# The front of a hybrid decoder block in two halves of the model width

## The chip, the cores and the metric

The kernel runs on one core of a Trainium2 chip. The metric is the device time of one execution in microseconds, from a program's start to its end; lower is better. The core has five engines that run side by side, each with its own instruction order: TensorE (PE) for matrix products and transposes, VectorE (DVE), ScalarE (ACT), GpSimd (POOL) and SyncE (SP), which issues nearly all of the DMA transfers. Engines wait for each other by semaphores.

## What is computed

The reference is one residual layer for 1024 positions and a model width of 1024, in float32:

```python
mod = (silu(c) @ w_ada + b_ada)                     # 6 rows of 1024
sh1, sc1, g1, sh2, sc2, g2 = split(mod, 6)
h = rms_norm(x, norm1_g) * (1 + sc1) + sh1
proj = h @ w_in                                     # q 512, k 128, v 128, u 512 columns
q = rope(rms_norm(q, q_norm_g), cos, sin)           # angles = positions * inv_freq
k = rope(rms_norm(k, k_norm_g), cos, sin)
attn = sliding_window_attention(q, k, v, sinks)     # window 128
pooled = means of u over the last 2, 4, 8, 16 positions, minus u
pool_out = (pooled @ pool_w per group) * pool_scale
x = x + g1 * (concat(attn, pool_out) @ w_o)
h2 = rms_norm(x, norm2_g) * (1 + sc2) + sh2
x = x + g2 * (square(relu(h2 @ w1)) @ w2)
```

For this document the part that matters is everything up to the first projections: the rows shift 1 (`sh1`) and scale 1 (`sc1`) must be computed from the vector `c` and two parts of `w_ada` of 4 MB each before any `h` exists, and `h` is needed before the first product with `w_in`.

## The kernel before

**Tiles.** The positions are cut in 8 tiles of 128 (`NT` = 8, `P` = 128), the model width in 8 blocks of 128 (`KD` = 8, `NK` = 4 of them are a half). Products are made in three parts to keep float32 accuracy: every operand is split in a high part (`hi`, a cast on ScalarE or GpSimd to a rounded format) and a low part (`lo`, what the cast lost, a subtraction on VectorE), and TensorE adds hi·hi, lo·hi and hi·lo. So the weights `w_in` have `wih` and `wil`, in two column groups: `wu` (the 512 columns of u, 4 pieces of two blocks each) and `wqkv` (768 columns, 8 pieces of one block each); and each tile's `h` has a high and a low part in two halves of 512 of the model width.

**The modulation rows.** `w_ada`'s rows lie over the 128 partitions, 8 to a partition. VectorE runs over 8 pieces of 128x1024 per modulation row: `add_piece` multiplies a piece by a column of silu(c) and adds it (L1205 for the first piece, L1207 for the others) to an accumulator: `acc` for `sh1`, `acc_sc` (in the tile `squares`) for `sc1`. Each add counts up `mod_summed`. What is left is a sum over partitions: TensorE multiplies the accumulator's eight blocks by a column of ones (`column_sum`, L2076), one column in each, and VectorE adds the bias and makes `b1` and `a1`, per-partition shift and scale for the transposed x (`scale_1`, L1269 and L1272). Later modulation rows (the "jobs" sh2, sc2, g1, g2) are summed in the same way between the tiles' work by lists of piece numbers (`first_pieces`, `between_pieces`, `late_pieces`), all in `acc`, and turned at tiles 3 and 5.

**x.** ScalarE squares a tile (`square_x`, L720), GpSimd makes 1/rms (`root_x`, L1872), ScalarE scales (`scale_x`, L725), TensorE transposes (`turn_x`, L2056), and VectorE (`make_h`, L1281) and ScalarE (`make_h_half`, L734) apply `a1` and `b1` to one half each. `hi_h` (L744) casts, `lo_h` (L1287) subtracts; `h_hi` and `h_lo` count these.

**Order.** Every engine's instructions stand in the order in which its block of the program is written. SyncE loads the pieces of the list `stream` one after another into 12 buffers (4 named `raw`, 8 named `slots`), and each load waits until its buffer was used. In the kernel before the list is: 8 of sh1, 8 of sc1, 4 of wu, 8 of wqkv; the tiles x 0 and x 1 are loaded behind piece 7. VectorE sums in that order, then makes the low parts of the weights (`lo_wu` L1294, `lo_wqkv` L1300). The rotary angles (`angles`, L1215 to L1234) are made after the first q is there, and their sines on ScalarE. TensorE sums the columns of sh1 right when they are ready, transposes x 0 and x 1, and fills the time until sc1 is ready with transposes that nobody reads (`keep_clock(n, bank)`, n multiplications with the identity, L2073; in the profile one such multiplication is two records). Then it sums the columns of sc1, and the projections start: u of tile 0, q and kv of tile 0, u of tile 1 and so on, over the whole width. `pool_windows` (L2200) and `pool_out` (L2173) are the pooling branch, `turn_qk` the transposes of the first queries and keys. From tile 2 on one loop runs over the tiles.

**GpSimd** builds the pooling matrices `band` with selects (`band_of`, L1858 and L1861, and L1866), among them the special first 16 columns of tile 0, which it overwrites again when tile 0 is done.

## Time and profile before

| | us |
|---|---|
| median of 3 runs | 937.73 (936.92 to 937.75) |
| the profiled execution, in all | 939.17 |
| its span, first to last instruction | 937.4 |
| TensorE busy in the span | 915.0 (98%) |
| VectorE busy | 650.2 (69%) |
| ScalarE busy | 495.1 (53%) |
| GpSimd busy | 361.7 (39%) |
| mean granted TensorE clock | 0.996 |

The profile was taken of one execution, whose own time is 1.4 us above the median of the runs without one; 1.7 us of it lie around the span. TensorE is the engine to look at: in all of the span's forty slices but the first and the last its busy digit is 9. The first slice, 23 us long, is where it is mostly idle. A row of the timeline gives an instruction's start, its length, engine, line, operation, what it writes and reads, the count of like instructions in a row, and in brackets the idle time of the engine ahead of it with what ended that. Ends of matmuls are modelled, so the time from one start to the next is the better measure of a matmul's cost. The granted clock is the share of full speed: 1.00 is 2.4 GHz, 0.50 is 1.2 GHz.

### The profile page before, as it was taken

How to read it: one execution, taken by the hardware profiler on the slowest of the kernel's cores; microseconds unless marked ns; L12 is line 12 of the kernel's file. 1: busy time of each engine (PE TensorE's matmuls, PEld its weight loads, DVE VectorE, ACT ScalarE, POOL GpSimd, SP SyncE). 2: the span in 40 equal slices, each digit the busy share in tenths (PEclk: the TensorE clock that was granted, in tenths of full speed). 3: DMA queues.
4: the chain of work that ended last, by engine and by line, in shares of the span. 5: the costliest groups of instructions: out<-in, count | busy, mean ns of one | idle time of the engine just before them, and what ended most of it. 6: DMA issues, size and time to landing. Idle time of an engine off the chain costs nothing.

```text
span 937.4 us, 12606 instructions
## 1 busy us (share of the span) xinstructions
PE 915.0 (98%) x4387; PEld 765.5 (82%) x4387; DVE 650.2 (69%) x1001; ACT 495.1 (53%) x869; POOL 361.7 (39%) x347
## 2 busy tenths in 40 slices
PE   2999999999999999999999999999999999999998
PEld 2888888887888888888888888888888888888886
DVE  6978987888645778556555654445786666799896
ACT  2657888887655546554455544536334444333331
POOL 8162322243323446988888888721000000000000
PEclk9899999999999999999999999999999999999999
DMA  9943232235122423746555553349999538996772
GB/s 357 371 170 95 91 114 90 91 106 188 45 90 90 134 69 123 243 162 197 188 176 169 176 184 131 115 172 332 349 339 320 196 102 289 317 302 209 258 248 94
DMA packets 92271, 175.54 MB, mean 187 GB/s; under 512 B 9320, under 2 KB 26288, under 8 KB 92208
## 3 DMA queue, kind: packets, MB, share of 16 engines
q1 hardware_dynamic: 92096, 174.70, 55.0%
q8 instruction: 35, 0.57, 0.2%
q14 instruction: 28, 0.23, 0.1%
q10 hardware_dynamic: 112, 0.04, 0.0%
HBM read 136.95 MB, written 37.75 MB: 186 GB/s over the span
## 4 chain that ended last, share of the span: by engine, by line
PE 92%; DVE 4%; DMA 2%; SPq 1%; issue 1%; ACT 1%; POOL 0%; DVEq 0%
PE psum L2060 27%; PE psum L2062 27%; PE psum L2061 27%; PE psum L2056 3%; DMA raw<-in_w_ada 2%; PE psum L2154 1%; PE psum L2155 1%; PE psum L2158 1%; PE psum L2140 1%; DVE w_o_lo L1372 1%; PE psum L2230 1%; PE psum L2200 1%; PE psum L2173 1%; PE psum L2236 1%; DVE probs L1337 1%
## 5 line engine op out<-in xcount | busy, mean ns | idle before, releaser
L1115 ACT CAST down_operands<-down_raw 128x1024 fp32r<-128x1024 f32 x96 | 100.9, 1054 | 151.9 <-PE psum L2062 54.6
L2060 PE MATMUL psum<-down_operands 128*128 128x512 f32 x448 | 174.3, 389 | 0.0
L2061 PE MATMUL psum<-down_operands 128*128 128x512 f32 x448 | 174.3, 389 | 0.0
L2062 PE MATMUL psum<-down_operands 128*128 128x512 f32 x448 | 174.3, 389 | 0.0
L1775 DVE TENSOR_TENSOR down_operands<-down_raw,down_operands 128x1024 fp32r<-128x1024 f32 x93 | 112.5, 1220 | 19.5 <-ACT down_operands L1115 18.9
L2060 PE MATMUL psum<-h2T,w_operands 128*128 128x512 f32 x272 | 106.0, 390 | 0.1
L2062 PE MATMUL psum<-h2T,w_operands 128*128 128x512 f32 x272 | 105.9, 389 | 0.0
L2061 PE MATMUL psum<-h2T,w_operands 128*128 128x512 f32 x272 | 105.8, 389 | 0.0
L2060 PEld LDWEIGHTS psum<-down_operands 128*128 128x128 f32 x448 | 84.1, 188 | 17.6
L2062 PEld LDWEIGHTS psum<-down_operands 128*128 128x128 f32 x448 | 84.1, 188 | 17.4
L2061 PEld LDWEIGHTS psum<-down_operands 128*128 128x128 f32 x448 | 84.1, 188 | 17.3
L2012 POOL TENSOR_TENSOR w_operands<-raw,w_operands 128x512 fp32r<-128x512 f32 x56 | 84.2, 1505 | 35.6 <-ACT w_operands L1063 35.6
L2062 PE MATMUL psum<-t_sums_hi,w_operands 128*128 128x512 f32 x168 | 65.4, 389 | 0.0
L2060 PE MATMUL psum<-t_sums_hi,w_operands 128*128 128x512 f32 x168 | 65.4, 389 | 0.0
L2061 PE MATMUL psum<-t_sums_lo,w_operands 128*128 128x512 f32 x168 | 65.4, 389 | 0.0
L2060 PEld LDWEIGHTS psum<-h2T,w_operands 128*128 128x128 f32 x272 | 51.1, 188 | 11.1 <-issue 0.5
L2061 PEld LDWEIGHTS psum<-h2T,w_operands 128*128 128x128 f32 x272 | 51.1, 188 | 10.6
L2012 POOL TENSOR_TENSOR w_operands<-w_sums,w_operands 128x512 fp32r<-128x512 f32 x42 | 55.3, 1329 | 11.3 <-ACT w_operands L1063 11.3
L2062 PEld LDWEIGHTS psum<-h2T,w_operands 128*128 128x128 f32 x272 | 51.1, 188 | 10.5
L1063 ACT CAST w_operands<-w_sums 128x512 fp32r<-128x512 f32 x42 | 26.1, 623 | 55.9 <-PE psum L2062 52.5
L2060 PE MATMUL psum<-w_o_hi,mixT_hi 128*128 128x512 f32 x128 | 51.2, 400 | 0.0
L2062 PE MATMUL psum<-w_o_hi,mixT_lo 128*128 128x512 f32 x128 | 50.0, 391 | 0.0
(285 smaller groups left out, 1960.9 us busy)
## 6 DMA issues: line engine op xcount, KB each, us to landing
down_raw<-in_w_mlp_out SPq DMA_DIRECT2D x160, 256.0 KB, 4.3
down_raw<-act_scratch SPq DMA_DIRECT2D x112, 256.0 KB, 3.3
raw<-in_w_ada SPq DMA_DIRECT2D x32, 512.0 KB, 4.6
raw<-in_w_mlp_in SPq DMA_DIRECT2D x32, 512.0 KB, 5.0
act_scratch<-act_quads_a SPq DMA_DIRECT2D x64, 256.0 KB, 2.3
act_scratch<-act_quads_b SPq DMA_DIRECT2D x48, 256.0 KB, 3.6
slots<-in_w_ada SPq DMA_DIRECT2D x8, 512.0 KB, 10.6
xh<-in_x SPq DMA_DIRECT2D x8, 512.0 KB, 5.7
```

Of the source, the lines that this page charges most:

```text
L1063: nc.scalar.copy(w1op[:, w1_slot(b, name), 0, :, :], w1_quad(b, quad)).then_inc(w1_hi, 1)
L1115: nc.scalar.copy(o[:, 0, :, :], r[:, 0:2, :]).then_inc(op2_hi, 1)
L1337: ins = v.tensor_tensor_reduce(out=pr[:, kv, h, 0:w], in0=banks(4)[:, 256 * h:256 * h + w], in1=mask[:, m0:m0 + w], scale=1.0, scalar=-3e3 ...
L1372: v.tensor_tensor(wol[:, k, :], piece_at(place[("wo", k)]), woh[:, k, :].bitcast(F32), ALU.subtract).then_inc(wo_lo_dve, 1)
L1775: v.tensor_tensor(o[:, 1, :, :], r[:, 0:2, :], f32(o[:, 0, :, :]), ALU.subtract).then_inc(op2_lo_dve, 1)
L2012: g.tensor_tensor(o[:, 1, :, :], quad, o[:, 0, :, :].bitcast(F32), ALU.subtract).then_inc(w1_lo, 1)
L2056: return nc.tensor.transpose(o, i, ident[0:rows_, 0:rows_])
L2060: mm(o, wh, ah, start=first, stop=False, skip_group_check=adds)
L2061: mm(o, wh, al, start=False, stop=False, skip_group_check=adds)
L2062: return mm(o, wl, ah, start=False, stop=last, skip_group_check=adds)
L2140: ins = mm(o, qT[:, kv * G + h, :], k_, start=a == 0, stop=a == 1)
L2154: mm(bank(0), h[:, k, :], wih[:, k, QKV:IN], start=k == 0, stop=False)
```

## The change

What it does:

1. The first job is cut along the model width. The list `stream` now begins with 8 pieces of kind `mod`, each with the first 512 columns of shift 1 and the first 512 of scale 1 of one row block (two runs of 2 KB in each partition where there was one of 4 KB). Then come wu 0 and 1, wqkv 0 to 3, the second halves (`mod` 8 to 15), wqkv 4 to 7, wu 2 and 3. x 0 is loaded behind piece 2, x 1 behind wu 1; x 2 and x 3 behind the parameter rows.
2. VectorE sums the first halves in `acc` (shift left, scale right) and the second in `squares` (`sum_front`), the last piece of each in two cuts of 512. The cast of the positions stands behind piece 2 of the first half, the columns' copy and `angles` behind piece 3; `angles` makes its products with one instruction from a row of constants (`inv_row`) that GpSimd sets, where it had eight.
3. TensorE projects the first half of the width for tile 0 and tile 1 (u in banks 0 and 1, q in 6 and 4, kv in 3 and 5), then the second half of both. In the two gaps ahead of a half it runs fills, 27 and 8 in the first, 11 in the second, and eight column sums.
4. The high parts of wu 1, wqkv 1 and wqkv 3 are cast on GpSimd instead of ScalarE. The matrix of tile 0's first 16 columns gets a tile of its own (`band_first`), with four narrow products more in `pool_windows(0)`, and nothing is overwritten later. GpSimd makes the roots of x 0 and x 1 one by one.
5. The jobs sh2, sc2 and g1 have an accumulator each, their pieces come later in the lists, and their turns move from tiles 3 and 5 to tiles 4 and 6.

The core of the diff:

```diff
-        stream = [("sh1", k) for k in range(KD)]
-        stream += [("sc1", k) for k in range(KD)]
-        stream += [("wu", k) for k in range(KD // 2)]
-        stream += [("wqkv", k) for k in range(KD)]
+        stream = [("mod", k) for k in range(KD)]
+        stream += [("wu", 0), ("wu", 1)]
+        stream += [("wqkv", k) for k in range(NK)]
+        stream += [("mod", KD + k) for k in range(KD)]
+        stream += [("wqkv", k) for k in range(NK, KD)]
+        stream += [("wu", 2), ("wu", 3)]
...
-        JOB_LOADS = (4, 4, 4, 3, 4, 4, 1, 0)
+        JOB_LOADS = (4, 2, 3, 4, 4, 5, 2, 0)
+        job_sums = (slots[:, NT - 1, :], slots[:, NT - 2, :], acc[:, :])
+        POOL_CASTS = ((1,), (1, 3))
...
+            if kind == "mod":
+                half = k // KD
+                return wada[:, k % KD, 0:2 * D].rearrange("p (m d) -> p m d", m=2)[:, :, 512 * half:512 * half + 512]
...
             for n in range(first_job):
                 load(n)
-                if n == 7:
+                if n == 2:
                     load_x(0)
+                if n == place[("wu", 1)]:
                     load_x(1)
-            load_x(2)
...
+            load_x(2)
+            load_x(3)
...
             def load_x(t):
                 if t >= 2:
-                    sp.wait_ge(h_lo, 2 * (t - 1))
+                    sp.wait_ge(h_lo, h_step(t - 2, 1))
```

VectorE:

```diff
+            def sum_front(half):
+                sums = acc_sc if half else acc
+                for k in range(KD):
+                    if k >= 1:
+                        dve.wait_ge(mod_summed, front_summed(KD * half + k - 1))
+                    if k < KD - 1:
+                        add_piece(sums[:, :], ("mod", KD * half + k), k, mod_summed)
+                    else:
+                        a = landed(dve, ("mod", KD * half + k))
+                        for m in range(2):
+                            cut = slice(512 * m, 512 * m + 512)
+                            v.scalar_tensor_tensor(out=sums[:, cut], in0=a[:, cut], scalar=silu[:, k:k + 1],
+                                                   in1=sums[:, cut], op0=ALU.mult, op1=ALU.add).then_inc(mod_summed, 1)
+                    if half == 0 and k == 1:
+                        dve.wait_ge(rows_in, 16 * 4)
+                        v.tensor_copy(rows[64:72, :], posi[64:72, :]).then_inc(posf_ready, 1)
+                    if half == 0 and k == 2:
+                        dve.wait_ge(rows_turned, 1)
+                        v.tensor_copy(cols[:, :], psum[:, 0, 0:72]).then_inc(cols_ready, 1)
+                        angles()
+                    if half == 1 and k == 1:
+                        lo_h(1, 0)
...
-            first_pieces = ([], [], (5,), (8,), (12, 13), (16,), (18, 19), (22,))
-            between_pieces = ([], [], [], (9,), (14,), (17,), (20,), (23,))
-            late_pieces = ((0, 1, 2, 3), (4,), (6, 7), (10, 11), (15,), [], (21,), [])
+            first_pieces = ([], [], (2,), (5,), (9,), (13, 14), (18,), (22,))
+            between_pieces = ([], [], [], (6,), (10,), (15,), (19,), (23,))
+            late_pieces = ([], (0, 1), (3, 4), (7, 8), (11, 12), (16, 17), (20, 21), [])
```

TensorE:

```diff
+            for n, fill in ((3, 8), (4, 7)):
+                pe.wait_ge(mod_summed, n)
+                keep_clock(fill, 3)
+            turn_x(0)
+            for n, fill in ((5, 3), (6, 5), (7, 4)):
+                pe.wait_ge(mod_summed, n)
+                keep_clock(fill, 3)
             pe.wait_ge(mod_summed, KD)
-            for k in range(KD):
-                ins = column_sum(psum[:, k // 4, k % 4:k % 4 + 1], acc, k)
+            for k in range(NK):
+                ins = column_sum(bank(1)[:, k:k + 1], acc, k)
             ins.then_inc(mod_turned, 1)
-            turn_x(0)
-            pe.wait_ge(cols_ready, 1)
-            turn_x(1)
-            keep_clock(3, 2)
-            for n, fill in ((13, 4), (14, 4), (15, 2)):
+            pe.wait_ge(mod_summed, KD + 1)
+            for k in range(NK):
+                ins = column_sum(bank(2)[:, k:k + 1], acc, NK + k)
+            ins.then_inc(sc1_turned, 1)
+            keep_clock(8, 3)
...
+            project_u_half(0, 0)
+            turn_x(1, 0, NK)
+            project_qkv_half(0, 0, (q_part(0), kv_part(0)))
+            project_u_half(1, 0)
+            project_qkv_half(1, 0, (q_part(1), kv_part(1)))
+            keep_clock(4, 2)
+            for n, fill in ((15, 4), (16, 3)):
                 pe.wait_ge(mod_summed, n)
                 keep_clock(fill, 2)
+            for m in range(2):
+                pe.wait_ge(mod_summed, 2 * KD + 1 + m)
                 for k in range(NK):
+                    ins = column_sum(bank(2)[:, NK * m + k:NK * m + k + 1], acc_sc, NK * m + k)
+            ins.then_inc(sc1_turned, 1)
+            pe.wait_ge(b1_second, 1)
+            pe.wait_ge(a1_ready, 2)
+            turn_x(1, NK, KD)
+            project_qkv_second()
+            project_u_half(0, 1)
+            project_u_half(1, 1)
+            pe.wait_ge(u_kept, 1)
+            turn_x(2)
+            project_qkv_half(1, 1, (q_part(1),))
             pool_windows(0)
-            turn_x(2)
-            pe.wait_ge(q_gained, 1)
-            project(bank(6), 0, AW, 1).then_inc(q_done, 1)
+            project_qkv_half(1, 1, (kv_part(1),))
             pool_out(0)
```

On TensorE, the stretch from the last fills ahead of the last column sums to the first product of u. `mod_summed` counts VectorE's adds, `ones` is the column of ones; before:

```order
L2073 MATMUL psum<-ident 128x128 [waits mod_summed]
L2073 MATMUL psum<-ident 128x128
L2076 MATMUL psum<-ones,squares 128x1 [waits mod_summed]
L2076 MATMUL psum<-ones,squares 128x1 x3
L2076 MATMUL psum<-ones,squares 128x1 [waits mod_summed]
L2076 MATMUL psum<-ones,squares 128x1 x3
L2073 MATMUL psum<-ident 128x128 [waits mod_taken]
L2073 MATMUL psum<-ident 128x128 x3
L2230 MATMUL psum<-w_in_hi,hT_hi 128x512 [waits wu_hi,h_hi]
```

and after:

```order
L2145 MATMUL psum<-ident 128x128 [waits mod_summed]
L2145 MATMUL psum<-ident 128x128 x3
L2148 MATMUL psum<-ones,acc 128x1 [waits mod_summed]
L2148 MATMUL psum<-ones,acc 128x1 x3
L2148 MATMUL psum<-ones,acc 128x1 [waits mod_summed]
L2148 MATMUL psum<-ones,acc 128x1 x3
L2145 MATMUL psum<-ident 128x128 x8
L2309 MATMUL psum<-w_in_hi,hT_hi 128x512 [waits wu_hi,cols_ready,h_hi]
```

The eight sums are now of half the shift and half the scale, and the fills behind them are eight and wait for nothing.

On TensorE after the change, the gap between the two halves; the rows ahead of it are the last products of the first half of tile 1, the rows behind it the second half of q and kv of tile 0. No such place is there before:

```order
L2315 MATMUL psum<-w_in_lo,hT_hi 128x256
L2145 MATMUL psum<-ident 128x128 x4
L2145 MATMUL psum<-ident 128x128 [waits mod_summed]
L2145 MATMUL psum<-ident 128x128 x3
L2145 MATMUL psum<-ident 128x128 [waits mod_summed]
L2145 MATMUL psum<-ident 128x128 x2
L2148 MATMUL psum<-ones,squares 128x1 [waits mod_summed]
L2148 MATMUL psum<-ones,squares 128x1 x3
L2148 MATMUL psum<-ones,squares 128x1 [waits mod_summed]
L2128 MATMUL psum<-ident,xh 128x128 [waits x_scaled,a1_ready,b1_second]
L2128 MATMUL psum<-ident,xh 128x128 x3
L2309 MATMUL psum<-w_in_hi,hT_hi 128x512 [waits wqkv_hi,h_front_hi]
```

Between a product of the first half and one of the second now stand 11 fills, eight column sums and four transposes of x tile 1, with three waits for VectorE's sums and one for shift and scale.

On VectorE, from the second piece to the point at which the first sums are done; `rows_in` counts the small rows (biases, gains, positions) that arrive on ScalarE's queue. Before, piece 2 to the columns' copy:

```order
L1207 SCALAR_TENSOR_TENSOR acc<-raw,small,acc 128x1024 [waits raw_in1,mod_summed]
L1207 SCALAR_TENSOR_TENSOR acc<-raw,small,acc 128x1024 [waits raw_in2,mod_summed]
L1207 SCALAR_TENSOR_TENSOR acc<-raw,small,acc 128x1024 [waits raw_in3,mod_summed]
L1207 SCALAR_TENSOR_TENSOR acc<-slots,small,acc 128x1024 [waits raw_in4,mod_summed]
L1251 CAST probs<-probs 8x128 [waits rows_in]
L1207 SCALAR_TENSOR_TENSOR acc<-slots,small,acc 128x1024 [waits raw_in5,mod_summed]
L1207 SCALAR_TENSOR_TENSOR acc<-slots,small,acc 128x1024 [waits raw_in6,mod_summed]
L1207 SCALAR_TENSOR_TENSOR acc<-slots,small,acc 128x1024 [waits raw_in7,mod_summed]
L1255 COPY cols<-psum 128x72 [waits rows_turned]
```

and after:

```order
L1257 SCALAR_TENSOR_TENSOR acc<-raw,small,acc 128x1024 [waits raw_in1,mod_summed]
L1300 CAST probs<-probs 8x128 [waits rows_in]
L1257 SCALAR_TENSOR_TENSOR acc<-raw,small,acc 128x1024 [waits raw_in2,mod_summed]
L1304 COPY cols<-psum 128x72 [waits rows_turned]
L1264 TENSOR_TENSOR probs<-cols,probs 128x64 [waits ident_made,cols_ready]
L1268 TENSOR_SCALAR probs<-probs 128x64 [waits own_dve]
L1270 TENSOR_SCALAR probs<-probs 128x64 [waits own_dve]
L1273 SCALAR_TENSOR_TENSOR probs<-probs 128x64 [waits own_dve] x3
```

The wait for the small rows moved from behind piece 5 to behind piece 2, and the angles from behind the first q to behind piece 3.

## Rows read from the trace of the kernel before

**Rows 1.** The page: busy time, the chain that ended last, one group of DMA issues.

```profile
PE 915.0 (98%) x4387; PEld 765.5 (82%) x4387; DVE 650.2 (69%) x1001; ACT 495.1 (53%) x869; POOL 361.7 (39%) x347
...
PE 92%; DVE 4%; DMA 2%; SPq 1%; issue 1%; ACT 1%; POOL 0%; DVEq 0%
...
down_raw<-act_scratch SPq DMA_DIRECT2D x112, 256.0 KB, 3.3
```

**Rows 2.** Waits of TensorE from 60 to 240 us: total, times, longest.

```profile
PE psum L2056 <- DVE kT L1367: 0.5, 1, 0.5
```

**Rows 3.** Timeline of TensorE and its weight loads: start, length, line, in brackets idle.

```profile
20.57 3.68 PE L2056 MATMUL psum<-ident,xh 128*128 128x128 f32 x16 [0.81 <-ACT xh L725]
...
26.29 0.97 PEld L2073 LDWEIGHTS psum<-ident 128*128 128x128 f32 x8 [0.35 <-DVE squares L1207]
...
28.39 1.95 PE L2076 MATMUL psum<-ones,squares 128*128 128x1 f32 x16
...
31.95 2.07 PE L2230 MATMUL psum<-w_in_hi,hT_hi 128*128 128x512 f32 x4 [0.61 <-ACT hT_hi L744]
...
40.38 0.50 PE L2230 MATMUL psum<-w_in_hi,hT_hi 128*128 128x512 f32 x2
...
47.80 0.51 PE L2230 MATMUL psum<-w_in_hi,hT_hi 128*128 128x512 f32 x2
...
48.85 0.40 PE L2154 MATMUL psum<-w_in_hi,hT_second 128*128 128x512 f32 x1
...
54.31 1.14 PE L2200 MATMUL psum<-band,u_rows 128*128 128x144 f32 x8
55.28 1.04 PE L2056 MATMUL psum<-ident,xh 128*128 128x128 f32 x8
...
65.41 0.81 PE L2056 MATMUL psum<-ident,qkn 128*128 128x128 f32 x6
```

**Rows 4.** Windows: length; busy PE, PEld, DVE, ACT, POOL; granted clock, DMA share, GB/s.

```profile
26.00:28.00 2.00, 1.68 (x13) 1.36 (x12) 1.93 (x3) 0.00 (x0) 1.88 (x3) 1.00 1.03 385
31.00:32.00 1.00, 0.39 (x5) 0.20 (x3) 0.96 (x4) 0.90 (x3) 0.00 (x0) 0.64 1.07 398
32.00:33.00 1.00, 1.00 (x3) 0.81 (x4) 1.00 (x2) 1.00 (x4) 0.00 (x0) 0.50 1.03 399
38.00:39.00 1.00, 1.00 (x5) 0.77 (x4) 1.00 (x2) 1.00 (x3) 0.00 (x0) 0.95 1.03 402
```

**Rows 5.** Timeline of VectorE.

```profile
6.35 1.28 DVE L1207 SCALAR_TENSOR_TENSOR acc<-raw,small,acc 128x1024 f32<-128x1024 f32 x1 [0.53 <-DMA raw<-in_w_ada]
...
11.97 0.22 DVE L1251 CAST probs<-probs 8x128 f32<-8x128 int32 x1
...
27.59 1.42 DVE L1247 SCALAR_TENSOR_TENSOR squares<-raw,small,squares 128x512 f32<-128x512 f32 x2
...
51.71 0.20 DVE L1220 TENSOR_SCALAR probs<-probs 128x64 f32<-128x64 f32 x1
...
53.66 0.20 DVE L1234 TENSOR_SCALAR probs<-probs 128x64 f32<-128x64 f32 x1
...
149.66 1.39 DVE L1366 TENSOR_TENSOR qT<-psum,qT 64x512 fp32r<-64x512 f32 x2 [1.62 <-ACT kT L817]
```

**Rows 6.** Issue of the last small row; loads issued from 2 to 3 us, time to landing.

```profile
3.74 0.36 ACTq L713 DMA_DIRECT2D probs<-in_positions  x1
...
raw<-in_w_ada SPq DMA_DIRECT2D x3, 512.0 KB, 5.7
```

**Rows 7.** Timeline of ScalarE.

```profile
31.80 1.50 ACT L734 ACTIVATE xh<-psum,small 128x128 f32<-128x128 f32 x4
```

**Rows 8.** Timeline of GpSimd.

```profile
10.74 1.25 POOL L1861 TENSOR_SCALAR_AFFINE_SELECT band<-band 128x16 f32<-128x16 f32 x1
...
16.98 0.20 POOL L1861 TENSOR_SCALAR_AFFINE_SELECT band<-band 128x16 f32<-128x16 f32 x1
...
201.97 1.04 POOL L1918 CAST w_o_hi<-raw 128x1024 fp32r<-128x1024 f32 x1 [5.62 <-PE psum L2062]
```

482 lines of the change are left out of this document (259 added, 223 removed).

## The prediction

> **What bounds the kernel now.** I read the page's busy shares and chain first: TensorE works in 98% of the span, and 92% of the chain that ended last is TensorE [rows 1]. The waits of the matmul queue from 60 to 240 us are four, 1.3 us together; the longest, 0.5, is for the low half of a key tile [rows 2]. So a microsecond taken out of the front counts in full, and one added counts in full. Next comes TensorE's timeline of the front [rows 3]. The first product starts at 31.95, and the transposes of the first queries and keys (turn_qk of tile 0) at 65.41. Both programs do the same work before that transpose, so its start is my yardstick. The windows [rows 4] show the third thing: the granted clock falls in the slice from 31 (0.64), is 0.50, the 1.2 GHz level, in the six whole microseconds behind it (the first is shown), and is back (0.95) in the slice from 38; before and after it is 2.4 GHz. The 24 products of u for tile 0 took from 31.95 to about 40.4, 8.43 us; the same 24 for tile 1 took 48.85 to 54.31, 5.46 us [rows 3]. The low clock costs the kernel before 3.0 us.
>
> What did the engine do before the clock fell? From 28.39 it ran the eight column sums, 1.95 us, which stream one column each; then four fills; then it was idle for 0.61 us [rows 3].
>
> **Part 1, the early start.** The new first job is eight pieces holding the first 512 columns of shift and scale. VectorE takes 1.28 us a piece [rows 5]. The pieces are cut in 2 KB rows instead of 4 KB. The nearest rows are the stretch in which the projection weights, also in 2 KB rows, arrive: 385 GB/s [rows 4], that is 1.36 us for 512 KB. VectorE, with its work of 1.30 a piece and what is added below, sets this stretch. It now waits for the small rows after piece 2. The last of them is issued at 3.74 to 4.10, and loads issued in that microsecond took 5.7 us to land [rows 6]; VectorE reached the same instruction only at 11.97 and did not wait [rows 5]. The wait ends between 7.8, where VectorE is ready anyway, and 9.8; I take 8.6, since these rows are small. With the cast and piece 3: 10.15. Then the angles: nine steps from 51.71 to 53.86 and a first one of 0.25 [rows 5], 2.4 us, and the copy of the columns 0.23: 12.8. They cost nothing where they stood, since TensorE's rows behind them, at 54.31 and 55.28, show no idle time [rows 3]; here they are on the path. Four pieces of 1.30 and two halves of 0.71 [rows 5]: the first sums stand at 18.7 and 19.4.
>
> TensorE's fills must not be late for them. A fill is two records in the profile and costs 0.24 us at the high clock (eight loads, four fills, in 0.97). The sixteen transposes from 20.57 ran at 0.23 us each, eight at 55.28 at 0.13 [rows 3]; at the slower of these rates a fill costs 0.43. The eight fills at 10.2 are done by 12.1 or 13.6, in any case before piece 4 is added at 14.1. The remaining 19 fills and eight transposes (0.87) take 5.5 us from 14.1 to 19.6, 0.9 us after the first half sum is ready, so the first column sums end at 20.6, the second at 21.6 (eight in 1.95, [rows 3]). Scale and bias: 0.45. ScalarE's four activations 1.50 [rows 7] and a cast 0.62: the first product starts at **24.2**, 7.7 us earlier. If the fills and transposes run at the slow rate up to there, add 1.5 us.
>
> **Part 2, the first half of the products.** Half of u is 12 products at 0.2275 us (5.46 / 24): 2.73. Half of q and kv is four steps of 1.05 (47.80 to 48.85): 4.2 [rows 3]. Two tiles: 13.9 us, and four transposes of x tile 1, 0.45. Tile 1's scaling waits for ScalarE's square (1.25), GpSimd's root (two small steps; I take 0.8) and the scaling (1.15) behind tile 0's cast: 27.65, against 27.0 on TensorE, a wait of 0.65. The casts of weights 1 and 3 go to GpSimd. A cast of 1024 columns took it 1.04 us [rows 8], so 0.8 for 768. The upper end is 2.1, with a VectorE instruction (1.28) in its way: the same select took 1.25 us beside VectorE's sums and 0.20 without [rows 8]. With the upper value VectorE ends its four low parts at 31.5, with the lower at 30.4; TensorE's fourth step is due at 31.3, so the cover just holds, and if it does not it is 0.2. First half done: 24.2 + 13.9 + 0.45 + 0.65 = **39.2**.
>
> **Part 3, the gap between the halves.** VectorE: 0.75, six pieces of 1.30, lo_h of tile 1 0.61, two halves 1.42: 10.6 us after 31.5, so 42.1. (The loads would allow 36.2: from a first landing at 5.1, sixteen pieces and two of wu at 1.36, two x tiles at 1.28, four of wqkv at 0.99, and 1.4 for the last piece's sum.) TensorE runs 11 fills, 2.7 us, to 41.9, then eight column sums, 1.95: 43.85. Shift and scale 0.5, two transposed blocks on VectorE 0.7 (four took ScalarE 1.50, [rows 7]), a cast of 256 columns 0.4: TensorE resumes at **45.6**. Of 6.4 us between the halves nothing is useful work. That is the price of the early start.
>
> **Part 4, to the yardstick.** q and kv of tile 0 4.2 and 0.35 of waiting for its low half; u twice, 5.46; then keep_u(0), which stands on ScalarE behind the square and scaling of x tile 2. That load now waits for three low halves (47.4) and lands after 3.3 (the fastest loads on the page, [rows 1]) to 5.7 us [rows 6]; I take 5.0, so u is kept at 56.2 and TensorE waits 0.6. Transposes 0.87, q of tile 1 2.73, pool windows 1.2 (0.97 from 54.31 to 55.28 [rows 3], plus four narrow matmuls), kv 1.45, pool products 0.9. Together 17.8: **63.4** at the high clock throughout, against 65.4 before. So the reordering gives 2.0 us, with the high clock granted everywhere.
>
> **Part 5, the steady part.** Three modulation pieces less before tile 2, three more behind it, and the two transposes of sums go from tiles 3 and 5 to 4 and 6. VectorE's path to the low part of q and k changes by -1.0, +0.2, +1.3 and +0.4 us at tiles 3 to 6 (pieces of 1.28 moved across it). At tile 5 it stood still 1.62 us ahead of that low part before [rows 5], and TensorE is 0.9 us later itself at tiles 4 and 6. I take 0, bounds -0.5 and +0.5 (its longest wait there, [rows 2]). The band that was mended after tile 0 (12 small GpSimd steps) goes away off the path: 0. The loads of x tiles 2 and 3 on SyncE now stand behind the parameters, and the job loads behind both; the first job piece is used only after norm_k(1): 0.
>
> **The clock, where I had to choose.** What preceded the fall at 31.3 is found twice in the new program: 1.95 us of column sums before each restart. At the second one no fill follows them; they are joined by the 1.6 us of shift, scale and cast in which TensorE has nothing but four transposes. At the first, eight fills follow, and 19 stand ahead. By the rows, the second restart is emptier than the stretch that preceded the fall before, so I expect the fall there: 3.0 us lost, of which waits of 0.35 and 0.6 in that stretch swallow about 0.5. At the first restart I take the high clock, as the fills are denser than before.
>
> The Trainium skill (TensorE: Matmul & The Clock Gate, "HAM oscillation — how this bites in real kernels") puts such falls down to idle gaps, waits for data between bursts of matmuls. By that rule the new gaps, each under 2 us of idleness and filled, would leave the clock high, and the sum would be the 935.7 of the first rival below; this trace speaks against it, since the clock fell behind column sums and one idle piece of 0.61 us.
>
> **The sum.** -2.0 (Parts 1 to 4) + 0 (Part 5) + 2.5 (one fall) = +0.5 us. The profiled execution took 939.17 with a span of 937.44, so 1.73 lie around the span; its plain runs have a median of 937.73. The sum makes the span 937.9, the profiled execution 939.7, and the median 937.73 + 0.5 = **938.2**.
>
> **The rivals.**
> First, the clock stays high over both restarts. For it: 19 and 11 fills and a split of the first column sums. Against it: 3.6 us in the second gap without any fill. It gives -2.0: 935.7.
> Second, the other side: the clock falls at both restarts. The first fall costs 3.0 less the 0.65 of waiting in the first half, 2.4 us. For it: 1.95 us of column sums and 0.7 us of nothing ahead of the first product, as before. Against: more fills. It decides only where TensorE and not VectorE ends the first half: beyond 0.65 us of loss every further one counts until the first half ends after 39.2, and from there it moves the whole second half, since 11 fills then run into the column sums. Total +2.9: 940.6.
> Third, the change brings no early start, because the small rows or GpSimd's root come late (upper bounds of Parts 1 and 2): up to 2 us later at 24.2, all of it kept. With one fall, 940.2.
>
> **How the numbers follow.** Chances: one fall 0.38, none 0.35, two 0.22, late start or anything else 0.05. Each case has about 1.3 us either way (0.8 from the small rows, 0.8 from the load of x tile 2 and the casts, 0.5 from Part 5, not all at once). The range reaches from 935.7 - 1.3 = 934.4 to 940.6 + 0.6 = 941.2; the likeliest case alone would be 936.9 to 939.5. A measurement of this kernel can tell about 0.2%, 1.9 us, from no change: faster is below 935.85, half of the first rival and a little of the likeliest and of the unknown, 0.27; slower is above 939.6, most of the second and third rivals and a little of the likeliest, 0.26; within is 0.47.
>
> **What would show it.** First product near 24.2 and the yardstick at 63.4 plus the half-clock loss. Part 1 is wrong if the first column sums begin away from 19.6; Part 2 if the first half ends away from 39.2, or if products wait for the casts of GpSimd; Part 3 if VectorE's last half sum is not near 42.1 or the restart not near 45.6; the clock choice if the granted clock does not fall near the second restart, or falls near the first. The prediction fails as a whole if the stretch behind the yardstick does not have the length that it had before.

## The result

The changed kernel takes 940.32 us (median of 10 runs, 938.43 to 941.34), the kernel before 937.11 us (10 runs, 936.56 to 937.75). The ratio is 1.0031, 95% interval 1.0022 to 1.0041: 0.31% slower, 2.9 us by the ratio and 3.2 between the two medians. The prediction said 938.2 with a range of 934.4 to 941.2 and 0.26 for slower by over 0.2%. So the range held, the likeliest value was 2.1 us too low, and the case that came is one to which I gave a quarter. For the profiled executions the forecast was closer: 939.7, and 940.24 came.

### The profile after

The page of the changed kernel, its busy times and its chain [rows 1]:

```profile
PE 919.8 (98%) x4453; PEld 770.5 (82%) x4453; DVE 647.8 (69%) x988; ACT 495.8 (53%) x875; POOL 353.7 (38%) x331
...
PE 92%; DVE 4%; ACT 1%; issue 1%; DMA 1%; POOL 1%; ACTq 0%; DVEq 0%
```

TensorE works 4.8 us more, in a span that is 1.1 us longer: what was added are 29 fills (46 in the two gaps against 17 before) and four narrow products. Its timeline of the front (the columns as in [rows 3]):

```profile
10.55 3.78 PE L2145 MATMUL psum<-ident 128*128 128x128 f32 x16 [0.87 <-DVE acc L1257]
14.53 2.66 PE L2145 MATMUL psum<-ident 128*128 128x128 f32 x14 [0.19 <-DVE acc L1257]
17.02 1.04 PE L2128 MATMUL psum<-ident,xh 128*128 128x128 f32 x8
...
20.57 1.84 PE L2148 MATMUL psum<-ones,acc 128*128 128x1 f32 x16
22.28 2.03 PE L2145 MATMUL psum<-ident 128*128 128x128 f32 x16
25.06 1.20 PE L2309 MATMUL psum<-w_in_hi,hT_hi 128*128 128x512 f32 x4 [0.75 <-ACT hT_hi L785]
...
34.93 1.20 PE L2312 MATMUL psum<-w_in_hi,hT_second 128*128 128x512 f32 x4 [0.45 <-DVE hT_second L1351]
...
40.66 2.62 PE L2145 MATMUL psum<-ident 128*128 128x128 f32 x22
43.11 1.84 PE L2148 MATMUL psum<-ones,squares 128*128 128x1 f32 x16
45.52 0.63 PE L2128 MATMUL psum<-ident,xh 128*128 128x128 f32 x4 [0.57 <-DVE small L1317]
46.73 2.70 PE L2309 MATMUL psum<-w_in_hi,hT_hi 128*128 128x512 f32 x8 [0.58 <-ACT hT_hi L792]
...
65.82 0.82 PE L2128 MATMUL psum<-ident,qkn 128*128 128x128 f32 x6
```

Read it against the forecast. The first column sums start at 20.57 (19.6 was forecast), the first product at 25.06 (24.2), the first half ends at 40.66 (39.2), the second column sums start at 43.11, products resume at 46.73 (45.6), and turn_qk(0), the yardstick, starts at 65.82 (63.4 at the high clock, 65.9 with the fall). The two waits of the second gap, 0.57 and 0.58, and the 0.45 ahead of the product with tile 1's low half, are all there is of idle time behind the first product but for some 0.3 us ahead of the transposes of x tile 1.

The windows of the changed kernel (columns as in [rows 4]) show where the granted clock fell:

```profile
47.00:48.00 1.00, 1.00 (x5) 0.83 (x5) 1.00 (x2) 1.00 (x3) 0.00 (x0) 0.51 0.06 16
...
50.00:51.00 1.00, 1.00 (x6) 0.86 (x5) 1.00 (x2) 1.00 (x4) 0.00 (x0) 0.78 0.88 328
```

It fell to 1.2 GHz once, right behind the second restart, as the forecast had chosen, but for 3.4 us (from 47.02, by the 0.51, to 50.44, by the 0.78) and not for the 6.8 us of [rows 4].

VectorE (columns as in [rows 5]):

```profile
8.96 0.22 DVE L1300 CAST probs<-probs 8x128 f32<-8x128 int32 x1 [0.85 <-DMA probs<-in_positions]
...
13.20 1.27 DVE L1257 SCALAR_TENSOR_TENSOR acc<-raw,small,acc 128x1024 f32<-128x1024 f32 x1
...
18.55 1.42 DVE L1296 SCALAR_TENSOR_TENSOR acc<-slots,small,acc 128x512 f32<-128x512 f32 x2
...
41.39 1.41 DVE L1296 SCALAR_TENSOR_TENSOR squares<-slots,small,squares 128x512 f32<-128x512 f32 x2
```

The small rows let it go at 8.96 (8.6 was forecast), the piece behind the angles began at 13.20 (12.8), the first sums stood at 19.3 and 20.0 (18.7 and 19.4) and the second half's at 42.8 (42.1).

So VectorE's steps were met within 0.7 us. TensorE's first column sums came 1.0 us late and the first half took 0.6 us more (15.6 for 15.0), and yet the yardstick is where the forecast with one fall had it, 65.8 for 65.9: the fall cost less than I had put down for it, and the errors cancelled. That match is luck. The experiments say where the 2.1 us of the median come from.

### The profile page after: what moved, and what is told of

Its sections match the earlier page's. It is cut to its first block, busy times and chain, and to the rows that moved or that the text cites. A ratio compares the mean times of both kernels' runs of the same rounds, so it can differ in the third digit from the quotient of the medians.

```text
span 938.5 us, 12724 instructions
## 1 busy us (share of the span) xinstructions
PE 919.8 (98%) x4453; PEld 770.5 (82%) x4453; DVE 647.8 (69%) x988; ACT 495.8 (53%) x875; POOL 353.7 (38%) x331
## 4 chain that ended last, share of the span: by engine, by line
PE 92%; DVE 4%; ACT 1%; issue 1%; DMA 1%; POOL 1%; ACTq 0%; DVEq 0%
PE psum L2132 26%; PE psum L2134 26%; PE psum L2133 26%; PE psum L2128 3%; PE psum L2213 1%; PE psum L2145 1%; PE psum L2312 1%; PE psum L2229 1%; PE psum L2309 1%; PE psum L2230 1%; PE psum L2233 1%; PE psum L2315 1%; DVE w_o_lo L1441 1%; PE psum L2249 1%; DVE probs L1406 1%
## 5 line engine op out<-in xcount | busy, mean ns | idle before, releaser
L2134 PE MATMUL psum<-t_sums_hi,w_operands 128*128 128x512 f32 x168 | 65.4, 389 | 0.0
L2132 PE MATMUL psum<-t_sums_hi,w_operands 128*128 128x512 f32 x168 | 65.4, 389 | 0.0
L2133 PE MATMUL psum<-t_sums_lo,w_operands 128*128 128x512 f32 x168 | 65.4, 389 | 0.0
```

Of the source, the lines that this page charges most:

```text
L2132: mm(o, wh, ah, start=first, stop=False, skip_group_check=adds)
L2133: mm(o, wh, al, start=False, stop=False, skip_group_check=adds)
L2134: return mm(o, wl, ah, start=False, stop=last, skip_group_check=adds)
```

## The experiments

All came from three questions. What is different between the executions? What holds the first column sums? What does the steady part cost? My theory after the first traces: TensorE's rate, and not the terms of the sum, makes most of the difference between forecast and time, and the turn that moved from tile 3 to tile 4 makes 0.8 us. The rival: the new order itself is longer on VectorE, in the front and in the steady part. The times of each comparison are against the kernel before on the same chip.

Two numbers are read from each trace and collected here, with the start of the first column sums and the first product: the distance from those sums to the start of turn_qk(0), and the distance from turn_qk(0) to turn_qk(6), which stands for the steady part. (The expectation of old_job_lists calls the end of this stretch turn_qk(7). The 126.4 and 127.2 that it gives reach to turn_qk(6), at 193.00 in the changed kernel; turn_qk(7) follows at 214.64. Measured to there the difference is the same, 148.8 against 148.1.)

| kernel | first sums | first product | turn_qk(0) | sums to turn_qk(0) | turn_qk(0) to (6) | granted clock at 0.50 |
|---|---|---|---|---|---|---|
| before | | 31.95 | 65.41 | | 126.43 | 31.3 to 38.1 |
| before_again | | 31.69 | 63.88 | | 126.41 | 32.3 to 35.7 |
| before_more_fills | | 32.60 | 63.99 | | 126.50 | 30.9 to 34.4 |
| after | 20.57 | 25.06 | 65.82 | 45.25 | 127.18 | 47.0 to 50.4 |
| after_again | 21.64 | 26.12 | 65.70 | 44.06 | 127.15 | none |
| early_fills | 21.56 | 26.05 | 66.45 | 44.89 | 127.21 | 16.2 to 19.6, 46.9 to 50.3 |
| second_gap_fills | 20.36 | 24.84 | 64.39 | 44.03 | 127.19 | none |
| old_job_lists | 19.86 | 24.53 | 65.41 | 45.55 | 126.54 | none |
| fewer_fills | 19.16 | 24.39 | 64.25 | 45.09 | 127.14 | 20.8 to 24.2, 44.7 to 48.1 |
| fewer_fills_act_cast | 19.41 | 24.00 | 64.77 | 45.36 | 127.21 | 22.3 to 25.8, 46.2 to 49.6 |
| dummy_turns | 19.96 | 24.62 | 64.12 | 44.16 | 127.60 | none |
| gap_fills_fewer_first | 21.59 | 26.08 | 65.67 | 44.08 | 127.18 | none |
| late_angles | 17.56 | 22.36 | 61.95 | 44.39 | 127.15 | none |
| no_gap_fills | 22.25 | 26.73 | 67.85 | 45.60 | 127.18 | 46.8 to 53.7 |

### The kernel before, once more

> The kernel before once more, unchanged, for a second trace. Its profiled execution was 1.4 to 2 us above its plain runs, and carried one fall of the granted clock (31.3 to 38.1) that cost 3.0 us. Theory A (which executions have a fall differs from one to the next): this trace shows the fall elsewhere, shorter, or not at all, and its span is then 935 to 936. Theory B (the fall belongs to the program): the same fall at 31.3, span 937.4 within 0.3. Time: 1.000 of the kernel before.

Measured: 937.69 (11 runs) against 937.34 (29 runs), ratio 1.0003, interval 0.9994 to 1.0012, as two times the same kernel must give. The new trace has a span of 935.8 instead of 937.4. Its windows:

```profile
32.00:33.00 1.00, 1.00 (x4) 0.82 (x3) 1.00 (x3) 1.00 (x3) 0.00 (x0) 0.64 1.03 399
...
35.00:36.00 1.00, 1.00 (x4) 0.76 (x4) 1.00 (x2) 1.00 (x2) 0.00 (x0) 0.66 1.02 396
```

and its yardstick:

```profile
63.88 0.82 PE L2056 MATMUL psum<-ident,qkn 128*128 128x128 f32 x6
```

Here the clock is low for 3.4 us and not for 6.8, and turn_qk(0) starts at 63.88, 1.5 us earlier than in [rows 3]. This is theory A, and it corrects the base of my sum. Of the 29 executions of the kernel before in this comparison, 17 had a mean clock of 0.998 like this trace and 937.1 to 938.3, 10 had 0.999 or 1.000 and 936.5 to 937.3, and 2 had 0.996, at 939.0. In all three comparisons together it is 45, 33 and 11 of 89. The trace that I read in advance, 939.17 in all and 0.996, is of the last and rarest kind. The 3.0 us of low clock that I put on the account of the kernel before are 1.5 by these two traces in its median execution, and less by the plain runs: in each of the three comparisons the executions with 0.998 have a median 1.1 us above those with 0.999 or 1.000, and those with 0.996 one 2.4 to 2.5 us above them.

### The changed kernel, once more

> The changed kernel once more, unchanged, for a second trace. Its ten runs spread over 2.9 us (938.43 to 941.34) at a mean clock that is 1.000 both in short and in long ones. Theory A (the slow start of TensorE, before its rate doubles, differs in length): the products start between 24.5 and 27.5, and the difference of the span from 938.5 is found ahead of the first product. Theory B (the second gap differs): the first product stays at 25.1 within 0.2 and the spread is behind 40 us. Ratio to before 1.003.

Measured: 939.84 (10 runs, 938.61 to 941.01), ratio 1.0026, interval 1.0017 to 1.0035. TensorE of this trace:

```profile
10.22 3.79 PE L2145 MATMUL psum<-ident 128*128 128x128 f32 x16 [0.87 <-DVE acc L1257]
14.71 3.36 PE L2145 MATMUL psum<-ident 128*128 128x128 f32 x14 [0.70 <-DVE acc L1257]
17.86 1.27 PE L2128 MATMUL psum<-ident,xh 128*128 128x128 f32 x8
...
21.64 1.84 PE L2148 MATMUL psum<-ones,acc 128*128 128x1 f32 x16
...
65.70 0.82 PE L2128 MATMUL psum<-ident,qkn 128*128 128x128 f32 x6
```

No fall of the clock at all, and yet turn_qk(0) starts only 0.1 us earlier than in the first trace. The time went at the other end, as theory A had it: the column sums start 1.07 us later, at 21.64. Nothing was idle ahead of them. The difference is in the rate of the fills: the fourteen records from 14.71 took 3.15 us up to the next row, against 2.49 in the first trace (14.53 to 17.02), and the eight transposes behind them 1.10 against 0.87. In both traces the first sixteen records took 3.78 us, twice what sixteen records behind the column sums need (2.03). The granted clock reads 1.00 in all these windows, but the trace's own record of it begins only at 16.3 in the one execution and at 18.3 in the other, and a window without a record prints 1.00. The durations say the same: the excess of the fourteen records and the eight transposes over the 1.67 us and 0.87 us that they take at the full rate (old_job_lists, below) is half of the time spent at the slow rate, which ends near 16.2 in the one and near 18.1 in the other. In the six traces with the same 27 fills the first column sums start between 19.86 and 22.25.

### Fills from the start

> The changed kernel with twelve more fills at the very start, from about 3.2 us until the small rows are there (8.9). Theory A (the low rate of the first fills delays the first column sums now and then): TensorE reaches its high rate before 10.6, the eight fills and seven fills are done long before the sums, the first column sums start at 19.3 instead of 20.57, and the time falls by 1 to 3 us, with a smaller spread. Theory B (the start is set by VectorE alone): first product 0.6 to 1.2 us earlier at most, spread as before.

Measured: 940.08 (8 runs), ratio 1.0024, interval 1.0014 to 1.0035, as the changed kernel. TensorE of this trace:

```profile
10.19 2.05 PE L2145 MATMUL psum<-ident 128*128 128x128 f32 x16 [0.87 <-DVE acc L1257]
14.70 2.03 PE L2145 MATMUL psum<-ident 128*128 128x128 f32 x14 [2.46 <-DVE acc L1257]
...
21.56 1.84 PE L2148 MATMUL psum<-ones,acc 128*128 128x1 f32 x16
```

```profile
16.00:17.00 1.00, 1.00 (x8) 1.00 (x7) 1.00 (x1) 0.00 (x0) 0.00 (x0) 0.59 1.05 385
...
19.00:20.00 1.00, 1.00 (x9) 1.00 (x7) 1.00 (x2) 0.00 (x0) 0.75 (x1) 0.70 1.01 395
```

The rate is high from 10.19 on (sixteen records in 2.05), as was hoped. But then the eight fills are done too soon, TensorE is idle for 2.46 us ahead of 14.70, and the granted clock falls at 16.2 for 3.4 us, in the middle of the next fills. The sums start at 21.56, no earlier than without. The expectation that they would start at 19.3 fell. The trace is of the longest of the eight executions, though: the four with a mean clock of 0.998, which have room for one fall only, took 938.3 to 939.8, the four with less (two falls or longer ones) 940.4 to 941.0. So an early full rate may have helped where the first fall did not come, which no trace shows. What the trace shows is that the early fills did not keep the clock: a fall followed the idle piece of 2.5 us behind them.

### Fills in the waits of the second gap

```diff
             ins.then_inc(sc1_turned, 1)
+            for _ in range(2):
+                mm(psum[:, 3, 256:256 + P], ident[:, :], ident[:, :], start=False, stop=False, skip_group_check=True)
             pe.wait_ge(b1_second, 1)
             pe.wait_ge(a1_ready, 2)
             turn_x(1, NK, KD)
+            for _ in range(2):
+                mm(psum[:, 3, 256:256 + P], ident[:, :], ident[:, :], start=False, stop=False, skip_group_check=True)
```

> The changed kernel with two fills behind the second column sums and two behind the transposes of x tile 1, in the two waits of 0.57 and 0.58 us of the second gap. Theory A (idle time and thin work in the gap let the clock fall): no fall at 47.0 to 50.3, the yardstick turn_qk(0) 1.5 us earlier than 65.82, time lower by up to 1.5. Theory B (the fall is not decided there): the fall stays, time within 0.3 us of the changed kernel; the fills themselves cost nothing or up to 0.2.

Measured: 938.86 (11 runs), ratio 1.0015, interval 1.0006 to 1.0024, which is 1.0 us under the changed kernel's median beside it. The intervals of the two overlap (1.0017 to 1.0035 there), so the times alone do not prove the gain. TensorE's second gap in this trace:

```profile
44.61 0.69 PE L2403 MATMUL psum<-ident 128*128 128x128 f32 x4
...
45.78 0.61 PE L2408 MATMUL psum<-ident 128*128 128x128 f32 x4
46.53 1.99 PE L2309 MATMUL psum<-w_in_hi,hT_hi 128*128 128x512 f32 x8
...
64.39 0.82 PE L2128 MATMUL psum<-ident,qkn 128*128 128x128 f32 x6
```

The two waits are gone, the clock stays high, and the sums-to-turn_qk(0) distance is 44.03 instead of 45.25. In all 11 executions the mean clock was 0.999 or 1.000; of the 20 of the unchanged kernel, 10 were at 0.998 or below. Theory A holds: four fills that cost nothing keep the clock. By the traces the price of the fall is 1.2 us where it comes (45.25 against 44.06 in the unchanged kernel). Its plain runs don't show this price: the ten executions with 0.999 or 1.000 have a median of 940.4, the ten with less 939.6. The start of the first sums, which no mean clock tells, differs by more than the fall costs.

### No fills in the second gap

```diff
-            keep_clock(4, 2)
-            for n, fill in ((15, 4), (16, 3)):
-                pe.wait_ge(mod_summed, n)
-                keep_clock(fill, 2)
```

> The changed kernel without the eleven fills of the second gap, so that TensorE is idle from 40.7 until the second half's sums are ready at 42.1. Theory A (the granted clock follows the idle and thin stretch ahead of a restart): a fall at the restart in nearly every run, 3.4 us long at least, mean clock 0.998 or less, and 0.7 to 1.5 us more than the changed kernel. Theory B (the fills are late work themselves): the column sums start at 42.1 instead of 43.1, and the time falls by up to 1.0.

Measured: 940.04 (9 runs), ratio 1.0027, interval 1.0017 to 1.0037, beside 1.0026 and 1.0031 of the changed kernel. The trace:

```profile
43.88 1.95 PE L2148 MATMUL psum<-ones,squares 128*128 128x1 f32 x16 [1.38 <-DVE squares L1296]
```

```profile
46.00:47.00 1.00, 0.61 (x4) 0.42 (x4) 0.87 (x5) 0.00 (x0) 0.00 (x0) 0.92 0.00 0
...
53.00:54.00 1.00, 1.00 (x6) 0.86 (x6) 1.00 (x4) 0.93 (x2) 0.00 (x0) 0.66 0.00 0
```

Six of nine executions have a mean clock of 0.996 and the others 0.998, so a fall came in all nine, and in this trace, of the longest of the nine executions, it is 6.8 us long (from 46.84, by the 0.92, to 53.68, by the 0.66; it is 0.50 in the slices between). That is theory A. But theory B is right beside it: the column sums start 17.15 us after the first product, against 18.05 in the changed kernel (25.06 to 43.11), 0.9 us sooner. The eleven fills are late work themselves: they end at 43.1 where VectorE's first half sum is there at 42.1. The two about cancel in the median. I had expected 0.7 to 1.5 us more; it is 0.2 or less.

The Trainium skill (TensorE: Matmul & The Clock Gate, "HAM oscillation — how this bites in real kernels") has the clock fall when TensorE waits for data between bursts. The traces agree as far as this: more idle time ahead of a restart makes the fall longer and surer (1.38 us of idleness ahead of the column sums and a fall of 6.8 us here, no idleness and no fall with the gap's fills). In the unchanged kernel, the same 0.6 us waits in the same place led to a fall in some executions and to none in others, which no rule on the program alone can give.

### Fewer fills ahead of the first sums

```diff
-            for n, fill in ((3, 8), (4, 7)):
+            for n, fill in ((3, 8), (4, 5)):
...
-            for n, fill in ((5, 3), (6, 5), (7, 4)):
+            for n, fill in ((5, 2), (6, 3), (7, 2)):
```

> The changed kernel with seven of the nineteen fills behind the first eight left out (5, 2, 3, 2 in place of 7, 3, 5, 4). Theory A (the fills themselves, and not VectorE's sums, are what the first column sums wait for): these start at 19.3 to 20.0 instead of 20.4 to 21.6, the first product at 24.0 to 24.6 instead of 24.8 to 26.1, and the time falls by 1 to 1.4 us. Theory B (VectorE's sums set it): first product as before within 0.2. Against both: the clock falls ahead of the sums because TensorE now has idle time there, as it did with the early fills (16.6 to 19.7), and 0.5 to 1.5 us are lost again.

Measured: 939.28 (12 runs, 937.62 to 941.43), ratio 1.0022, interval 1.0011 to 1.0034. The trace:

```profile
19.16 2.13 PE L2148 MATMUL psum<-ones,acc 128*128 128x1 f32 x16
21.16 3.47 PE L2145 MATMUL psum<-ident 128*128 128x128 f32 x16
24.39 1.18 PE L2309 MATMUL psum<-w_in_hi,hT_hi 128*128 128x512 f32 x4
```

```profile
20.00:21.00 1.00, 1.00 (x10) 1.00 (x10) 0.16 (x1) 0.00 (x0) 0.67 (x1) 0.89 1.04 402
...
24.00:25.00 1.00, 1.00 (x8) 0.91 (x7) 0.61 (x1) 1.00 (x3) 0.00 (x0) 0.90 1.05 387
```

The column sums start at 19.16, so the fills had held them: VectorE's first half sum stands at 19.07 here. About half of the 1.4 us gained on the first trace of the changed kernel is then lost again (the first product is 0.7 us earlier), since the clock falls at 20.8, at the end of the column sums, and the eight fills behind them take 3.23 us up to the first product, against 2.03 for the same sixteen records in the changed kernel and 0.75 of waiting. TensorE goes from them to that product without a wait: the fills hold it now. Both theories got their part, and the remark against both as well. The runs show it too: those with a mean clock of 1.000 took 937.62 to 938.79, those with 0.994 about 941. But two with 0.998 took 941.3 and 941.4 and two with 0.996 only 938.7 and 939.0, so the clock of the trace is not all of the spread. Against the changed kernel the gain of the median is not clear of noise (its ratios were 1.0026 and 1.0031).

### The same, with wu 1 cast on ScalarE

```diff
-        POOL_CASTS = ((1,), (1, 3))
-        HI_COUNT = ((1, 1, 2, 3), (1, 1, 2, 2, 3, 4, 5, 6))
+        POOL_CASTS = ((), (1, 3))
+        HI_COUNT = ((1, 2, 3, 4), (1, 1, 2, 2, 3, 4, 5, 6))
...
             hi_wu(0)
+            hi_wu(1)
             make_h_half(0, 0)
...
-            hi_wu_second()
```

> As the kernel with fewer fills, and the high part of wu 1 cast on ScalarE, which was idle for 3.6 us there, instead of GpSimd. Theory A (GpSimd's cast at 19.2 and VectorE's last two half sums stand in each other's way: 2.19 us in place of 1.42 in two of four traces): the half sums take 1.42 in this trace, and with TensorE no longer late the median falls by another 0 to 0.8 us and the spread shrinks. Theory B (ScalarE's cast comes too late for u): products of u wait at their third, first half longer by up to 0.5.

Measured: 939.32 (12 runs, 937.88 to 940.48), ratio 1.0019, interval 1.0011 to 1.0028: no difference from the kernel with fewer fills that can be told. Theory A was right on the sums and wrong on their weight. VectorE's two last half sums took 1.42 us here. Five of the seven traces with the cast on GpSimd and no fill left out of the first gap show them at 2.19 or 2.20, among them after_again:

```profile
18.65 2.19 DVE L1296 SCALAR_TENSOR_TENSOR acc<-slots,small,acc 128x512 f32<-128x512 f32 x2
```

```profile
19.20 1.10 POOL L1950 CAST w_in_hi<-slots 128x1024 fp32r<-128x1024 f32 x1 [5.79 <-DMA slots<-in_w_in]
```

In the first trace of the changed kernel it is the other way round, 1.42 on VectorE and 1.27 on GpSimd:

```profile
19.59 1.27 POOL L1950 CAST w_in_hi<-slots 128x1024 fp32r<-128x1024 f32 x1 [3.48 <-DMA slots<-in_w_in]
```

Whichever engine comes second in that microsecond waits. In old_job_lists and dummy_turns, where the column sums would have been ready for it, this cost 0.2 us (2.03 and 2.02 us from start to end for the sixteen records instead of 1.84). In the others TensorE was later than VectorE anyway.

### The old lists of pieces and turns

```diff
-        JOB_LOADS = (4, 2, 3, 4, 4, 5, 2, 0)
+        JOB_LOADS = (4, 4, 4, 3, 4, 4, 1, 0)
...
-            late_pieces = ([], (0, 1), (3, 4), (7, 8), (11, 12), (16, 17), (20, 21), [])
+            late_pieces = ((0, 1, 2), (3, 4), (6, 7), (10, 11), (15,), [], (21,), [])
...
             lo_h(2, 1)
+            add_job_pieces(late_pieces[0])
             add_carry(0)
...
-                if t in (4, 6):
+                if t in (3, 5):
```

> The changed kernel with the pieces of the jobs and the turns of their sums back where they were before (turns at tiles 3 and 5; the first five pieces 3 + 2 around tile 0 and 1). Theory A (the turn at tile 3 lies in TensorE's wait for the key's low half and costs nothing there, at tile 4 it costs its 0.8 us): the stretch from the start of turn_qk(0) to that of turn_qk(7), 127.2 us in four traces of the changed front and 126.4 in two of the kernel before, goes back to 126.4, the wait ahead of x tile 4's transposes from 1.36 to 0.5; ratio to before 1.0018. Theory B (the lists of pieces delay VectorE's path and the turn does not matter): the stretch stays at 127.2 or grows, by the three pieces that VectorE does ahead of tile 1's sums.

Measured: 940.39 (11 runs), ratio 1.0029, interval 1.0019 to 1.0038. TensorE's waits from 60 to 240 us in this trace (columns as in [rows 2]):

```profile
PE psum L2129 <- DVE carry L1459: 1.2, 1, 1.2
PE psum L2129 <- DVE kT L1436: 0.5, 1, 0.5
```

The steady part goes back to 126.54 and the wait for kT to 0.5: theory A. But the time does not fall, for a reason outside both theories: the three pieces that VectorE now adds ahead of add_carry(0) hold up turn_qk(0) by 1.2 us. Before the change, VectorE had that time. In the new order it does not, and the later lists are the price of the new front.

This trace also has the earliest first sums of the six with 27 fills:

```profile
14.64 1.83 PE L2146 MATMUL psum<-ident 128*128 128x128 f32 x14 [0.82 <-DVE acc L1257]
...
19.86 2.03 PE L2149 MATMUL psum<-ones,acc 128*128 128x1 f32 x16
```

The nineteen fills and eight transposes behind piece 4 all ran at the full rate here, in 5.22 us (the fourteen records in 1.67, the transposes in 0.87), and the sums still followed them without a pause, 0.6 us after VectorE's first half sum (19.3).

### Dummy turns at tiles 3 and 5

```diff
             for t in range(2, NT):
+                if t in (3, 5):
+                    pe.wait_ge(carry_kept, t)
+                    keep_clock(3, 1)
```

> The changed kernel with three fills (0.73 us) put in at the head of tile 3 and of tile 5, read by nobody. One look; read are the distances between the starts of turn_qk, 25.3 from tile 2 to 3 and 24.0 from tile 4 to 5 in four traces. Theory A (at tile 3 TensorE waits for the key's low half anyway, at tile 5 for nothing): the wait at tile 3 shrinks from 1.36 to 0.6 and its distance stays at 25.3 within 0.1, while the stretch over tile 5 grows by 0.7. Theory B (both tiles are bound alike): both grow by 0.7, or neither.

Measured, one execution: 939.04, span 937.2. The wait for kT:

```profile
PE psum L2128 <- DVE kT L1436: 0.7, 1, 0.7
```

It was 1.4 in the changed kernel:

```profile
PE psum L2128 <- DVE kT L1436: 1.4, 1, 1.4
```

From turn_qk(1) to turn_qk(3), with tile 3's fills in between, it is 40.74 us here (80.72 to 121.46) and 40.76 in the changed kernel (82.43 to 123.19): the three fills at tile 3 are free. (The wait for carry_kept that the edit adds does not show among TensorE's waits.) (They stand ahead of turn_qk(2), so the single distance that I named moved by 0.7, which the next one gave back.) Over tile 5, from turn_qk(3) to turn_qk(5), it is 47.33 against 46.89: 0.4 of the 0.7 are paid. So tile 3 has a hole of 1.4 us in TensorE's work, and what is taken out of it and put elsewhere is paid at least in part. The old order had the turn of sh2's sums there, the new one has it at tile 4, where no such hole is.

### More fills in the kernel before

```diff
-            keep_clock(4, 0)
+            keep_clock(7, 0)
```

> The kernel before with seven fills instead of four ahead of the first product, in the 0.62 us in which TensorE waits for the cast of h. Theory A (the fall of the granted clock near 32 follows the thin stretch of column sums and that wait): no fall in most runs, mean clock 1.000 in them, span 934.7, as the shortest runs of the kernel before had; ratio 0.9986. Theory B (the fall does not depend on these fills): ratio 1.000 within 0.0007, mean clock 0.998 as before.

Measured: 936.97 (11 runs) against 937.47 (35 runs), ratio 0.9996, interval 0.9987 to 1.0004. This is unclear; theory A's ratio of 0.9986 lies outside the interval. In the profiled execution the clock fell at 30.9 all the same, while the fills ran, and these filled more than the wait: the first product starts at 32.60, against 31.69 in before_again. Six of the 11 had a mean clock of 0.999 or 1.000, against 13 of 35 of the kernel before in the same comparison, a difference that chance can make. The long fall (0.996, five of the 35) did not come in the eleven, which may be chance.

### Fills in both places, three fewer ahead

> The changed kernel with the four fills in the second gap's waits, wu 1 cast on ScalarE, and three of the first gap's nineteen fills left out. Theory A (fills too many hold up the first sums, fills too few let the clock fall; three less is between): first column sums at 19.4 to 20.3, no fall of the clock in most runs, median 938.0 to 938.5, that is 0.4 to 0.9 below the kernel with the gap's fills alone (938.86), spread under 2 us. Theory B (density must be kept whole): falls return, median 938.9 or above.

It has second_gap_fills' four fills, the cast on ScalarE, and (4, 6) and (5, 3), (6, 4), (7, 3) as fills of the first gap. Measured: 938.28 (11 runs, 937.88 to 940.22), ratio 1.0010, interval 1.0001 to 1.0018, all executions at a mean clock of 0.999 or 1.000. The median and the clock are as in theory A; the spread, 2.3 us, is over the 2 that it allowed, and the sums start at 21.59 and not at 19.4 to 20.3. The trace is of the longest execution of the eleven: in it the high rate came late (its record begins at 19.2). I estimate that with that rate early they would start 1.5 to 2 us sooner, and the shortest execution is 2.3 us shorter; no trace shows it. Against second_gap_fills (1.0015) the intervals overlap, so what the three fills are worth can't be told.

### Angles back where they were

```diff
-                        angles()
...
                             poolw[:, :, :].rearrange("p g d -> p (g d)"), scale_row, ALU.mult).then_inc(poolw_ready, 1)
+            angles()
             norm_k(0)
...
             scale_x(0)
-            sines()
...
             keep_u(0)
+            sines()
...
-            for n, fill in ((3, 8), (4, 7)):
+            for n, fill in ((3, 3), (4, 3)):
...
-            for n, fill in ((5, 3), (6, 5), (7, 4)):
+            for n, fill in ((5, 1), (6, 2), (7, 4)):
```

> The changed kernel with angles and sines back behind the sums of q and k of tile 0, thirteen fills instead of 27 ahead of the first sums, wu 1 cast on ScalarE, and the four fills in the second gap. Theory A (the 2.8 us of angles ahead of piece 4 are on the path since VectorE's sums end the front): first column sums at 17.0 to 18.0, first product at 21.5 to 22.7, turn_qk(0) at 61.9 to 63.0, and if the clock holds a time of 936.3 to 937.3, at or under the kernel before. Theory B (ScalarE's sines and their table load, late, hold up the first queries and keys): first product early, but turn_qk(0) no earlier than 64.4; time 938 to 940. A lower density of fills may let the clock fall on top: 1.5 us each time.

Measured: 936.39 (11 runs, 936.13 to 936.78) against 937.58 of the kernel before (25 runs): ratio 0.9985, interval 0.9976 to 0.9994. This is faster than both kernels, by 1.2 us against the one and by 3.9 against the other's median of 940.32 (from another comparison). By the mean clocks, most of the 1.2 us is the clock: the ten executions of the kernel before with a mean clock of 0.999 or 1.000 in this comparison have a median of 936.73, and against them this kernel gains 0.3 us. TensorE of this trace:

```profile
17.56 1.84 PE L2148 MATMUL psum<-ones,acc 128*128 128x1 f32 x16
...
22.36 1.20 PE L2309 MATMUL psum<-w_in_hi,hT_hi 128*128 128x512 f32 x4 [1.07 <-ACT hT_hi L785]
...
61.95 0.82 PE L2128 MATMUL psum<-ident,qkn 128*128 128x128 f32 x6
```

VectorE's first sums:

```profile
16.58 1.41 DVE L1297 SCALAR_TENSOR_TENSOR acc<-slots,small,acc 128x512 f32<-128x512 f32 x2
```

and ScalarE's sines:

```profile
52.95 1.28 ACT L911 ACT_TABLE_LOAD   x1
55.37 0.70 ACT L911 ACTIVATE trig<-probs 128x64 f32<-128x64 f32 x4 [1.13 <-DVE probs L1283]
```

The column sums start at 17.56 and the first product at 22.36, 2.7 us ahead of the changed kernel's, and the distance from the sums to turn_qk(0), 44.39, is as in the other traces with a high clock (44.03 to 44.16) but for 0.3. VectorE's half sums start at 16.58 instead of 18.55. So the 2.5 us of angles (10.67 to 13.20 in the changed kernel), which cost nothing that shows at 53 us, held VectorE's sums up by 2.0 us at 10 us, and with them the fills, which wait for these sums. All eleven executions have a mean clock of 0.999 or 1.000, and their spread is 0.65 us instead of 2.9: with few fills ahead, the moment at which TensorE gets its full rate hardly decides the time any more. (In this trace the sums start 0.3 us after VectorE's first half sum is there.) The edits were made together; of the 1.9 us between this kernel and gap_fills_fewer_first (938.28), both on one chip, the part of the angles and that of the eleven further fills left out were not tried apart, though the one makes the other possible.

## Why the prediction was right or wrong

- **The yardstick of before.** The step that failed first is "-2.0: turn_qk(0) at 63.4 at the high clock throughout, against 65.4 before". The 65.4 holds a low clock of 6.8 us, the 63.4 none. With its fall taken out, the kernel before is at 65.41 - 3.0 = 62.4, and the reordering *costs* 1.0 us by my own numbers. (With the 2.4 us that a long fall costs by the plain runs it is at 63.0, and the reordering costs 0.4.) I then put +2.5 for the one fall of the new program, as long as the old one's, and had +0.5. That would have been sound for two executions with one long fall each. The median execution before has a short fall and stands at 63.88. Put on this base, my own terms give 63.4 + 1.2 to 1.5 - 63.9 = +0.7 to +1.0 instead of +0.5, so this step makes 0.2 to 0.5 of the miss. The 3.0 came from the 24 products of u alone (8.43 against 5.46); of the whole time a long fall takes the 2.4.
- **Part 1** had the right parts and one wrong bound. The small rows (8.96 for 8.6), the angles and the sums (19.3 and 20.0 for 18.7 and 19.4) were 0.3 to 0.6 late. The larger error is the sentence on TensorE's fills, "if the fills and transposes run at the slow rate up to there, add 1.5 us": I took the better end. The traces have the first sums at 19.86 to 22.25 instead of 19.6, always right behind the fills and not behind VectorE. That the fills end last was in the forecast (19.6 against 18.7); what it had too low is their time. In old_job_lists and dummy_turns they ran at the full rate from piece 4 on and the sums came 0.3 to 0.4 us late, with VectorE's steps; in the other four the slow rate lasted past piece 4 and cost up to 2.3 us more (no_gap_fills: 14.74 to 22.25, 7.51 us instead of 5.22), above the 1.5 that I had named. The mean of the six is 20.8, 1.2 us late, and this is the largest part of the miss.
- **Parts 2 to 4** were good. From the sums to turn_qk(0) I had 43.8 us; the traces with a high clock have 44.03 to 44.16. The first half was 15.6 us instead of 15.0, the gap 6.1 instead of 6.4, the rest 17.9 instead of 17.8 (46.53 to 64.39 in second_gap_fills). GpSimd's casts cost VectorE time (0.79 us of waiting in the first trace), within the bounds; how much of TensorE's wait of 0.45 for tile 1's low half comes from them was not tried. The working has one slip: 43.85 and the 1.6 us behind it give 45.45, not 45.6.
- **Part 5** failed: 0 forecast, +0.75 measured (127.14 to 127.21 in every trace with the new lists and turns and no dummy turns, against 126.41 to 126.50), outside my bound of 0.5. By the last sign that I named, a stretch behind the yardstick of another length, the prediction failed as a whole. I looked at VectorE's path per tile and forgot that the turn itself is 0.8 us of TensorE's time, and that at tile 3 it stood in front of the longest wait of the steady part, the 0.5 of [rows 2]. A wait of 0.5 with 0.8 of other work ahead of it is a hole of 1.3. After the change it is 1.36. That row was in my hand, and I used it as a bound only.
- **The clock** was right in place, and wrong in size. The fall came at the second restart, in 3.4 us instead of 6.8 and at 1.2 us instead of 2.5, in half of the executions. The rival without a fall was about as frequent. The second rival (two falls) did not show in either trace of the unchanged kernel, only where fills were moved or left out (early_fills, fewer_fills, fewer_fills_act_cast); one of its 20 executions, at 0.996 and 941.34, can have had two falls or a long one.
- **The sum** as it came, for the first trace against the second trace of before: first sums and all behind them up to turn_qk(0) +1.94 (65.82 - 63.88), steady part +0.77, together 2.7, which is the difference of the spans (938.5 - 935.8); the medians differ by 3.2 in one comparison and 2.5 in the other. Term by term, as an estimate from the figures above: +0.5 forecast, +0.2 to +0.5 from the base and the size of the fall, +1.2 from the first sums, +0.3 from there to the yardstick, +0.75 behind it, together +2.9 to +3.2 in an execution with a fall and 1.2 less in one without.

The chance of 0.26 for slower came from rivals that did not happen, and the range held because they had widened it: that is luck, too. The kernel became slower by the fills of the first gap and by the turn that lost its cover, and the forecast hid the rest of the loss by comparing a program without a fall with an execution that had a rare, long one.

## What to carry to other kernels

Before a difference is built on a yardstick in one trace, take what the clock did out of both sides; a profiled execution that is longer than all plain runs is a sign that it holds something rare. Fills are work: count them at the slow rate when TensorE has only just begun, and let them end well before the work behind them is due. Work like the angles that costs nothing where it stands should stay in that hole, and work that stands just ahead of a wait is free only there.

## What the runs showed of the hardware

TensorE's first fills ran at half rate for 3 to 9 us after they began at 10.2 to 10.6, in six traces of programs that are alike up to there (column sums from 19.86 to 22.25), while the granted clock of the windows reads 1.00 for want of a record; the durations tell (sixteen records in 3.78 us, later in 2.03).

GpSimd's cast of 1024 columns and VectorE's multiply-and-add with two inputs from the same memory held each other up: 1.42 and 1.27 us (or 1.54 in second_gap_fills) when VectorE was first, 2.19 and 1.04 to 1.15 when GpSimd was. The Trainium skill (GPSIMD Engine Reference, "Key points") says that GpSimd shares its memory interface with VectorE and contends with instructions that have two inputs there, and these rows agree.
